# Scores of the cached K pages on TensorE from transposed pages, and the issue of K and V pages between the engines' steps

## The chip, the cores and the metric

One Trainium2 chip, one core. The metric is the device time of one execution of the program in microseconds. Three runs of the kernel before gave 4904.9 to 4907.69, median 4907.25.

## What is computed

One inference step of a two-layer trunk, for a prompt of 1024 tokens and for 8 samples of one new token each, with the same weights. Layer 0 has stick-breaking attention (part A) and an RWKV-7 mixing (part B) side by side. For each sample, part A reads a paged cache of 8192 earlier tokens: 64 pages of K and 64 of V, 128 tokens x 8 heads x 64 each, in float32 (256 KB a page), at places that a page table names.

```python
z = einsum('bthd,bshd->bhts', q, past_k) * DH ** -0.5 + bias      # scores, 8 heads, 8192 tokens
u = log_sigmoid(-z);  after = reversed cumsum of u, less u
w = exp(log_sigmoid(z) + after)
o = einsum('bhts,bshd->bthd', w, past_v)
```

Part B runs over the prompt in chunks of 64 tokens; each chunk has a small triangular system per head, and its state goes from chunk to chunk.

## The kernel before

All in float32 on tiles of 128 partitions. The program is a series of phases with a barrier after each: load, norm, Q and K, V, `pb_phase` (the 14 tiles of B's projection, each 72 matmuls of 344 columns in three groups), `attention_phase` (the prompt's attention), `rwkv_phase`, output projection, FFN, then layer 1. The cached pages of the 8 samples are worked on beside `pb_phase` (scores of sample 0) and `rwkv_phase`. The order on each engine is written out by hand; engines meet at semaphores alone.

K pages. SyncE issues one page after another into a ring of 8 buffers (`load_key_page`, L1021: wait until the buffer is free, load the page's number from the table, issue). The query of a sample is turned once on TensorE, stored to DRAM and loaded back as a row on all partitions (`start_sp`, `load_q`). VectorE forms the scores of two pages in a unit (`keys_dve`, L1110): a product of 128 x 1024 with the query (L1119), then a sum over 64 within each head (L1123). After 32 units `bias_dve` adds the bias for all pages of the sample.

V pages. ScalarE issues them one by one into a ring of 8 (`load_values`, L1076, called from `fetch`), between its own steps. TensorE adds each page with the weights of its 128 tokens (8 columns) to one of four column positions of bank 7 (`values_pe`, L1050, L1058), in any gap where `more(n)` stands. Scores become weights through `logs_act`, `softplus_dve`, `sums_pe`, `exponents_dve`, `weights_act`; the four positions are added up by `fold_act`, `select_pe`, `pick_act`.

`rwkv_phase` has 8 pairs of chunks. In pair i the V pages of sample i and the K pages of sample i + 1 are handled; the last pair has no K pages. A pair is: the preparation (`prep_act`, `prep_dve`, `prep_pe`; first exponential L1535, decays L1570), `prepped`, the transposes (L1692), the spread copies (L1801), the Gram products (L1700), the copies of the transposes (L1804 to 1808), five levels of the solve (`solve_levels_*`: a product, its copy y on ScalarE at L1415, one or two more products, an update on VectorE; VectorE has four units of K per level, TensorE four V pages in each of two gaps, ScalarE's queue eight page issues after each copy of y), two halves of the state's recurrence (L1729 to 1753), the copy of o (L1824), the fold (L1098) and the end of the pair with four V pages for the next one. The first seven pairs are a loop.

In `pb_phase` SyncE loads the weights of tile t + 2 when the row work of tile t is done (`mixed`; the same buffer holds mu), ScalarE rounds them (L248), VectorE forms the rest (L253) and, after two units of K pages, does the row work (L936 to 939).

## Time and profile before

| | us |
|---|---|
| median of 3 runs | 4907.25 (4904.9 to 4907.69) |
| profiled execution: device time | 4906.5 |
| profiled execution: span | 4904.6 |
| busy in the span: PE matmul | 3996.3 (81%) |
| DVE | 2586.6 (53%) |
| ACT | 1226.2 (25%) |
| POOL | 242.0 (5%) |
| page products L1119 and sums L1123 on DVE | 316.2 + 312.9 |
| V products L1058 on PE | 381.2 |
| `pb_phase` | about 236 to 457 |
| `rwkv_phase` | 723 to about 1925 |

PE is TensorE's matmuls, DVE VectorE, ACT ScalarE, SP SyncE; a q behind the name is the engine's queue of instructions, where DMAs are issued and registers computed. A row of a timeline is: start in us from the span's start, length, engine, line, operation, written tile <- read tiles, shape, count, and in brackets the idle time before it and what ended it. Neighbouring instructions of one kind are merged into one row, whose length goes from the first start to the last end. A float32 matmul shows as two records. PEclk is the granted clock of TensorE as a share of full speed, 2.4 GHz.

### The profile page before, as it was taken

To read this page: it belongs to the slowest core of one execution; us is meant where nothing else is said; L and a number is where in the kernel's file an instruction comes from. 1 tells how busy PE (TensorE), PEld (TensorE's weight loads), DVE (VectorE), ACT (ScalarE), POOL (GpSimd) and SP (SyncE) were. 2 spreads that over 40 slices of the span, in tenths; PEclk is the share of its full clock that TensorE was granted. 3 is DMA by queue.
4 is the path that set the end of the run, shared out by engine and by line. 5 is a ranking of instruction groups with operands and counts; after the bars stand their busy time and mean duration, and the time that the engine had idled before them with its cause. 6 is when DMAs were issued, how large, how long until landed. Compare 5 with 4: busy or idle time off the path is not lost. (4 is left out here: it accounts for less than half of the span.)

```text
span 4904.6 us, 82685 instructions
## 1 busy us (share of the span) xinstructions
PE 3996.3 (81%) x29517; PEld 3334.2 (68%) x29517; DVE 2586.6 (53%) x3393; ACT 1226.2 (25%) x1915; POOL 242.0 (5%) x302
## 2 busy tenths in 40 slices
PE   6786887666667774699998969995887876999998
PEld 6685323233333333699998959994777766999998
DVE  2156887777888744234334425554666423433443
ACT  3211551122111122222223322232222212222232
POOL 0000000000000000000000000001011000000000
PEclk8898998877789876899999989996877888999999
DMA  2253007766787751311114532322111132111254
GB/s 94 70 156 121 26 33 261 232 216 221 234 276 253 243 168 64 121 44 43 44 43 144 160 116 88 94 82 81 32 36 44 54 138 78 43 45 50 74 159 137
DMA packets 288462, 566.18 MB, mean 115 GB/s; under 512 B 41425, under 2 KB 107345, under 8 KB 281658
## 3 DMA queue, kind: packets, MB, share of 16 engines
q1 hardware_dynamic: 182186, 375.32, 24.0%
q10 hardware_dynamic: 90000, 141.65, 9.0%
q0 software_dynamic: 16032, 45.92, 2.4%
q8 instruction: 157, 2.57, 0.2%
q14 instruction: 87, 0.71, 0.0%
HBM read 504.38 MB, written 58.79 MB: 115 GB/s over the span
## 5 line engine op out<-in xcount | busy, mean ns | idle before, releaser
L261 PE MATMUL ps<-ffn_hh,up_wh 128*128 128x344 f32 x2112 | 677.9, 321 | 59.5 <-DVE up_wl L253 59.5
L263 PE MATMUL ps<-ffn_hl,up_wh 128*128 128x344 f32 x2112 | 676.3, 320 | 0.0
L262 PE MATMUL ps<-ffn_hh,up_wl 128*128 128x344 f32 x2112 | 675.5, 320 | 0.0
L1058 PE MATMUL ps<-pg_v,pg_w 128*8 128x512 f32 x1024 | 381.2, 714 | 156.7 <-DMA pg_v<-in_v_pages 106.6
L261 PEld LDWEIGHTS ps<-ffn_hh,up_wh 128*128 128x128 f32 x2112 | 398.2, 189 | 60.5 <-issue 60.5
L262 PEld LDWEIGHTS ps<-ffn_hh,up_wl 128*128 128x128 f32 x2112 | 398.2, 189 | 0.0
L263 PEld LDWEIGHTS ps<-ffn_hl,up_wh 128*128 128x128 f32 x2112 | 398.1, 188 | 0.0
L459 PE MATMUL ps<-down_ah,down_wh 128*128 128x344 f32 x1056 | 345.4, 327 | 48.1 <-DVE down_al L495 28.7
L1119 DVE TENSOR_TENSOR pg_prod<-pg_k,pg_q 128x1024 f32<-128x1024 f32 x256 | 316.2, 1235 | 47.7 <-DVE rw_mxt L1430 13.5
L461 PE MATMUL ps<-down_al,down_wh 128*128 128x344 f32 x1056 | 339.1, 321 | 0.0
L460 PE MATMUL ps<-down_ah,down_wl 128*128 128x344 f32 x1056 | 338.9, 321 | 0.0
L1123 DVE TENSOR_REDUCE pg_z<-pg_prod 128x16 f32<-128x1024 f32 (+1 forms) x256 | 312.9, 1222 | 11.4
L253 DVE TENSOR_TENSOR down_wl<-down_w,down_wh 128x1408 fp32r<-128x1408 f32 x96 | 155.9, 1624 | 308.4 <-ACT down_wh L248 308.4
L1058 PEld LDWEIGHTS ps<-pg_v,pg_w 128*8 128x8 f32 x1024 | 45.5, 102 | 391.2 <-DMA pg_v<-in_v_pages 310.9
L261 PE MATMUL ps<-hh,odd_wh 128*128 128x344 f32 x792 | 254.4, 321 | 31.7 <-DVE odd_wl L253 31.7
L262 PE MATMUL ps<-hh,odd_wl 128*128 128x344 f32 x792 | 253.8, 320 | 0.0
L263 PE MATMUL ps<-hl,odd_wh 128*128 128x344 f32 x792 | 253.8, 320 | 0.0
L459 PEld LDWEIGHTS ps<-down_ah,down_wh 128*128 128x128 f32 x1056 | 199.7, 189 | 62.2 <-issue 50.8
L248 ACT ACTIVATE down_wh<-down_w 128x1408 fp32r<-128x1408 f32 x96 | 132.4, 1379 | 379.5 <-PE ps L461 351.7
L460 PEld LDWEIGHTS ps<-down_ah,down_wl 128*128 128x128 f32 x1056 | 200.7, 190 | 0.0
L461 PEld LDWEIGHTS ps<-down_al,down_wh 128*128 128x128 f32 x1056 | 199.9, 189 | 0.0
L664 DVE TENSOR_TENSOR ffn_a<-up_cv,ps 128x344 f32 (+1 forms) x132 | 67.4, 511 | 246.7 <-PE ps L263 246.7
(430 smaller groups left out, 7463.8 us busy)
## 6 DMA issues: line engine op xcount, KB each, us to landing
pg_k<-in_k_pages SPq DMA_DIRECT2D x512, 256.0 KB, 4.5
pg_v<-in_v_pages ACTq DMA_DIRECT2D x512, 256.0 KB, 4.6
down_w<-in_w_down SPq DMA_DIRECT2D x96, 704.0 KB, 4.2
up_w<-in_w_ff SPq DMA_DIRECT2D x44, 1034.0 KB, 4.9
odd_w<-in_w_odd SPq DMA_DIRECT2D x33, 512.0 KB, 3.8
scratch_odd_rows<-odd_cv POOLq DMA_DIRECT2D x32, 516.0 KB, 2.9
dn_x<-scratch_odd_rows SPq DMA_DIRECT2D x8, 1536.0 KB, 7.7
scratch_x<-out_x POOLq DMA_DIRECT2D x16, 516.0 KB, 2.9
```

Source lines behind the costliest of these rows:

```text
L248: act.activation(hi, w, ACT.Copy).then_inc(rounded, 1)
L253: dve.tensor_tensor(lo, w, hi.bitcast(F32), ALU.subtract).then_inc(rest_ready, 1)
L261: pe.matmul(out, wh, xh, start=(k == 0), stop=False)
L262: pe.matmul(out, wl, xh, start=False, stop=False)
L263: mm = pe.matmul(out, wh, xl, start=False, stop=(k == n - 1))
L459: pe.matmul(ps[:, j, 0:GC], wh[:, v, wk], ah[:, kk, :], start=(kk == 0), stop=False)
L460: pe.matmul(ps[:, j, 0:GC], wl[:, v, wk], ah[:, kk, :], start=False, stop=False)
L461: mm = pe.matmul(ps[:, j, 0:GC], wh[:, v, wk], al[:, kk, :], start=False, stop=(kk == FT - 1))
L664: dve.tensor_tensor(a[:, bass.ds(2 * i + j, 1), col].rearrange("p a t -> p (a t)"), cv[:, j, col], ps[:, 3 + c, 0:GC], ALU.mult).then_inc( ...
L1058: pe.matmul(self.T.ps[c:c + H_A, 7, :], wts[:, :, g], self.vp[:, n, :], start=(g < 4), stop=(g >= NPG - 4), tile_position=(0, c), skip_gro ...
L1119: dve.tensor_tensor(self.prod[:, :, :], self.kp[:, n:n + 2, :], self.q[:, :].unsqueeze(1).to_broadcast([P, 2, D_A]), ALU.mult).then_inc(se ...
L1123: dve.tensor_reduce(z.rearrange("p h n -> p n h"), self.prod[:, :, :].rearrange("p n (h d) -> p n h d", h=H_A), AX.X, ALU.add).then_inc(se ...
```

## The change

K pages lie transposed in DRAM: for each page 128 channels of a head pair on the partitions, four such blocks, 128 tokens in a row (`k_pages` of `layouts`); the bytes of a page and its 2 KB per partition are the same. The query is kept as a block matrix of 32 columns per channel block (`qa`, `qb`). TensorE forms the scores of eight pages in a *round* (`keys_pe`): four channel blocks one after another, in each four matmuls with 256 moving columns in four column positions, into bank 6. ScalarE copies 128 x 256 (`scores_act`), TensorE transposes them back in two parts (`turn_pe`), VectorE adds the bias (`bias_dve`, eight short ones per sample).

SyncE issues K pages by rounds into a ring of 16, with one wait for eight pages. ScalarE issues V pages in *groups* of four with one wait for four, and TensorE waits for all four of a group. The places of groups, rounds and turns in each engine's order are new; the loops of `pb_phase` are unrolled. In `rwkv_phase` several tiles share memory (yw with rw, ya with ra, eN with L, eX with t1, o, oc and rs with L, nm and t2), and V's ring is allocated there. The core of the diff:

```diff
-            with sp.Fori(1, NB_T // 2) as i:
+            sp.wait_ge(pages.table_in, 16)
+            pages.load_keys(sp, 0, 0)
+            for i in range(1, NB_T // 2):
                 weights(i, 0)
-                keys(i)
+                pages.load_keys(sp, 0, i)
                 weights(i, 1)
-            keys(NB_T // 2)
+            pages.load_keys(sp, 0, NB_T // 2)
...
-            with pe.Fori(0, NB_T // 2) as i:
+            for i in range(NB_T // 2):
                 for j in range(2):
                     pe.wait_ge(w_split, 2 * i + j + 1)
                     for c in range(GRP):
                         pe.wait_ge(row_in, 6 * i + 3 * j + c + 1)
                         group_products(pe, T, 3 * j + c, wh[:, j, :], wl[:, j, :], c).then_inc(product, 1)
+                    if j == 0:
+                        pages.keys_pe(pe, 0, i)
+                    else:
+                        pages.turn_pe(pe, 0, i)
+            pages.keys_pe(pe, 0, NB_T // 2)
+            pages.turn_pe(pe, 0, NB_T // 2)
...
-            with act.Fori(0, LAST) as i:
+            pages.start_act(act)
+            for i in range(LAST + 1):
                 tile(i, 0)
-                tile(i, 1)
-            tile(LAST, 0)
-            tile(LAST, 1, True)
+                pages.scores_act(act, 0, i)
+                tile(i, 1, i == LAST)
+            pages.scores_act(act, 0, LAST + 1)
...
-
-                first, units = (RING // 2 * j, RING // 4) if i is not LAST else (0, RING // 2)
-                for n in range(units):
-                    pages.keys_dve(dve, 0, i if i is not LAST else LAST + j, first + 2 * n)
                 dve.wait_ge(row_in, 6 * i + 3 * j + 3 + 6)
...
+    def load_keys(self, sp, b, r):
+        at = NPG * b + self.ROUND * r
+        sp.wait_ge(self.k_used, at + self.ROUND)
+        for n in range(self.ROUND):
+            slot = self.ROUND * (r % 2) + n
+            sp.dma_start(self.kp[:, slot, :, :], self.T.io["k_pages"][self.page(sp, at + n), :, :, :]
+                         .rearrange("a p c t -> (a p) c t")).then_inc(self.k_in[r % 2], 16)
+
+    def load_values(self, sp, b, q):
+        at = NPG * b + self.GROUP * q
+        sp.wait_ge(self.v_used, at + self.GROUP)
+        for n in range(self.GROUP):
+            sp.dma_start(self.vp[:, self.GROUP * (q % 2) + n, :], self.T.io["v_pages"][self.page(sp, at + n), :, :]
+                         .rearrange("a p n -> (a p) n")).then_inc(self.v_in[q % 2], 16)
...
+    def keys_pe(self, pe, b, r):
+
+
+        if r == 0:
+            pe.wait_ge(self.q_ready, b + 1)
+            if not (isinstance(b, int) and b == 0):
+                pe.wait_ge(self.z_ready, b)
+        if not (isinstance(b, int) and b == 0 and r == 0):
+            pe.wait_ge(self.biased, 8 * b + r)
+        pe.wait_ge(self.k_in[r % 2], 512 * b + 128 * (r // 2) + 128)
+        alone(pe, self.passed)
+        first = self.ROUND * (r % 2)
+        for c in range(4):
+            for j in range(4):
+                mm = pe.matmul(self.T.ps[32 * j:32 * j + 32, 6, 0:2 * PAGE], self.qb[:, c, :],
+                               self.kp[:, first + j:first + self.ROUND:4, c, :], start=(c == 0), stop=(c == 3),
+                               tile_position=(0, 32 * j), skip_group_check=True)
+        mm.then_inc(self.k_used, self.ROUND)
+
+    def turn_pe(self, pe, b, r):
+
+        pe.wait_ge(self.z_copied, 8 * b + r + 1)
+        for n in range(2):
+            mm = pe.transpose(self.T.ps[:, 6, (2 + n) * P:(3 + n) * P], self.zt[:, n * P:(n + 1) * P], self.T.const("ident"))
+        mm.then_inc(self.z_turned, 1)
...
+        for q in groups:
+            if q == 0:
                 pe.wait_ge(self.w_ready, b + 1)
-            n, c = g % self.RING, 32 * (g % 4)
-            pe.wait_ge(self.v_in[n], 16 * self.loads * b + 16 * (g // self.RING) + 16)
-            pe.matmul(self.T.ps[c:c + H_A, 7, :], wts[:, :, g], self.vp[:, n, :], start=(g < 4), stop=(g >= NPG - 4),
-                      tile_position=(0, c), skip_group_check=True).then_inc(self.v_used, 1)
+            pe.wait_ge(self.v_in[q % 2], 512 * b + 64 * (q // 2) + 64)
+            alone(pe, self.passed)
+            for j in range(self.GROUP):
+                mm = pe.matmul(self.T.ps[32 * j:32 * j + H_A, 7, :], wts[:, :, self.GROUP * q + j],
+                               self.vp[:, self.GROUP * (q % 2) + j, :], start=(q == 0), stop=(q == NPG // self.GROUP - 1),
+                               tile_position=(0, 32 * j), skip_group_check=True)
+            mm.then_inc(self.v_used, self.GROUP)
...
+    def next_q_act(self, act, b):
+        act.wait_ge(self.k_used, self.RING + NPG * b)
+        act.activation(self.qb[:, :, :].rearrange("p c x -> p (c x)"),
+                       self.qa[:, bass.ds(b, 1), :, :].rearrange("p a c x -> p (a c x)"), ACT.Copy).then_inc(self.q_ready, 1)
+
+    def scores_act(self, act, b, r):
+        act.wait_ge(self.k_used, self.RING + NPG * b + self.ROUND * (r + 1))
+        act.activation(self.zt[:, :], self.T.ps[:, 6, 0:2 * P], ACT.Copy).then_inc(self.z_copied, 1)
 
     def logs_act(self, act, b):
...
             act.sem_inc(S["k_rn"], 1)
-            if sample is not None:
-                fetch(12)
             act.wait_ge(S["l_ready"], i + 1)
             act.activation(cut(t["eL"], n), cut(t["L"], n), ACT.Exp, scale=-DECAY)
             act.activation(cut(t["eN"], n), cut(t["L"], n), ACT.Exp, scale=DECAY)
...
             pe.matmul(ps[:, 3, 0:4 * n], halves, cut(t["t1"], n), start=True, stop=True).then_inc(S["k_sum"], 1)
-            more(8)
+            more(2)
             pe.wait_ge(S["rkk"], i + 1)
             pe.matmul(ps[:, 4, 0:4 * n], halves, cut(t["t2"], n), start=True, stop=True).then_inc(S["bonus"], 1)
-            more(4)
+            more(1)
...
@@ -1681,9 +1680,19 @@
         @block.tensor
         def _(pe):
             pe.wait_ge(S["lora_in"], 16)
-            def pair(i):
-                read = iter(range(NPG))
+            def pair(i, keys=True):
+                read = iter(range(NPG // Pages.GROUP))
                 more = lambda n: pages.values_pe(pe, i, [g for _, g in zip(range(n), read)])
+                score = lambda r: pages.keys_pe(pe, i + 1, r) if keys else None
+                turn = lambda r: pages.turn_pe(pe, i + 1, r) if keys else None
+
+                def between(n):
+                    more(1)
+                    if n % 2:
+                        score(n // 2 + 1)
+                    else:
+                        turn(n // 2)
+
                 prep_pe(pe, i, W, sample=i, more=more)
                 pe.wait_ge(S["prepped"], i + 1)
                 pe.wait_ge(S["gate_copied"], i + 1)
@@ -1709,8 +1718,10 @@
                 pe.wait_ge(S["spread"], 3 * i + 3)
                 gram(3, t["K"], Rx)
                 gram(4, t["B"], Rx)
-                more(4)
-                solve_levels_pe(pe, T, S, i, mtl, xm, xt, y, (5, 2, 1), S["pe_passed"], lambda: more(4))
+                more(1)
+                score(0)
+                slots = iter(range(10))
+                solve_levels_pe(pe, T, S, i, mtl, xm, xt, y, (5, 2, 1), S["pe_passed"], lambda: between(next(slots)))
...
                         mm = pe.matmul(ps[q(hd), 4, oc_(hd // 2)], u[r, hc(hd)], rb[r, hc(hd)], start=False, stop=True,
                                        skip_group_check=True)
                     mm.then_inc(S["mixed"], 1)
-                    more(4)
+                    turn(5 + p)
+                    more(1)
+                    score(6 + p)
                 finish_pe(pe, i, o[:, :, :], W)
+                turn(7)
                 pages.select_pe(pe, i)
...
         @block.scalar
         def _(act):
             act.preload_act_table_set(EXP_LN_SET)
+            pages.load_values(act, 0, 0)
+            pages.load_values(act, 0, 1)
             act.dma_start(X[:, :, :], xs[:, :, 0:W]).then_inc(S["xs_in"], 16)
             act.wait_ge(S["cleared"], 1)
...
                         last = act.activation(dst[r, :, e, :], src[r, :, :], ACT.Copy)
                     last.then_inc(S["spread"], 1)
+                pages.load_values(act, i, 2)
+                pages.load_values(act, i, 3)
                 act.wait_ge(S["turned"], i + 1)
                 act.activation(ktm[:, :], ps[:, 5, :], ACT.Copy)
...
-                fetch(20)
-                solve_levels_act(act, T, S, i, y, (5, 2, 1), lambda lv: fetch(20 + 8 * lv))
+                pages.load_values(act, i, 4)
+                scores(0)
+                pages.load_values(act, i, 5)
+
+                def between(lv):
+                    pages.load_values(act, i, 2 * lv + 4)
+                    scores(lv)
+                    if lv < 5:
+                        pages.load_values(act, i, 2 * lv + 5)
+
+                solve_levels_act(act, T, S, i, y, (5, 2, 1), between)
                 for p in range(2):
                     r = slice(64 * p, 64 * p + 64)
                     act.wait_ge(S["w_done"], 2 * i + p + 1)
                     act.activation(r0[r, :], ps[r, 0, :], ACT.Copy).then_inc(S["w_copied"], 1)
                     act.wait_ge(S["u_done"], 2 * i + p + 1)
                     act.activation(u[r, :], ps[r, 5, :], ACT.Copy).then_inc(S["u_copied"], 1)
-                    fetch(NPG)
+                    if p == 0:
+                        pages.load_values(act, i, 15)
+                        scores(6)
                 act.wait_ge(S["mixed"], 2 * i + 2)
                 act.activation(o[:, :, :], ps[:, 4, :].rearrange("p (k w) -> p k w", k=4), ACT.Copy)\
                    .then_inc(S["o_copied"], 1)
+                scores(7)
+                if more_samples:
+                    pages.load_values(act, i + 1, 0)
+                    pages.load_values(act, i + 1, 1)
...
                 dve.sem_inc(S["masked"], 1)
-                solve_levels_dve(dve, T, S, loop, i, xm, xt, (5, 2, 1), lambda lv: more(1 if lv == 1 else 4))
+                solve_levels_dve(dve, T, S, loop, i, xm, xt, (5, 2, 1), lambda lv: bias(lv - 1))
...
                     last.then_inc(S["h_ready"], 1)
+                    bias(5 + p)
                 assert loop.n == 20, loop.n
-                more(1)
-                finish_dve(dve, i, o[:, :, :], W, h[:, 4:8, bass.ds(i * W, W)], more)
-                more(NPG)
+                finish_dve(dve, i, o[:, :, :], W, h[:, 4:8, bass.ds(i * W, W)])
+                bias(7)
```

## Rows read from the trace of the kernel before

**Rows 1.** Stages: length; busy (count) of PE, PEld, DVE, ACT, POOL; PEclk, DMA share, GB/s.

```profile
236.00:457.00 221.00, 172.79 (x1012) 168.76 (x1012) 129.32 (x120) 30.88 (x57) 15.63 (x30) 0.90 0.48 145
876.00:1023.00 147.00, 100.99 (x936) 49.17 (x936) 115.38 (x123) 26.44 (x50) 8.05 (x5) 0.83 0.73 238
924.00:982.00 58.00, 49.60 (x540) 18.15 (x536) 49.26 (x45) 2.99 (x5) 0.00 (x0) 1.00 0.96 329
1755.00:1858.00 103.00, 83.97 (x924) 42.46 (x923) 30.62 (x47) 21.60 (x37) 7.09 (x5) 0.91 0.54 156
```

**Rows 2.** Part 5 of the page: the page operations on DVE.

```profile
L1119 DVE TENSOR_TENSOR pg_prod<-pg_k,pg_q 128x1024 f32<-128x1024 f32 x256 | 316.2, 1235 | 47.7 <-DVE rw_mxt L1430 13.5
...
L1123 DVE TENSOR_REDUCE pg_z<-pg_prod 128x16 f32<-128x1024 f32 (+1 forms) x256 | 312.9, 1222 | 11.4
```

**Rows 3.** Timeline of ACT, then of DVE, in the projection of B.

```profile
259.06 0.46 ACT L907 ACTIVATE pb_row<-ps 128x344 f32<-128x344 f32 x1 [3.33 <-PE ps L263]
266.59 1.06 ACT L248 ACTIVATE pb_wh<-pb_w 128x1024 fp32r<-128x1024 f32 x1 [7.07 <-DMA pb_w<-in_w_pb]
...
270.40 0.46 ACT L907 ACTIVATE pb_row<-ps 128x344 f32<-128x344 f32 x1 [2.05 <-PE ps L263]
...
260.89 1.29 DVE L939 SCALAR_TENSOR_TENSOR pb_xs<-pb_xs,pb_w,pb_row 128x1032 f32<-128x1032 f32 x1
267.69 1.23 DVE L253 TENSOR_TENSOR pb_wl<-pb_w,pb_wh 128x1024 fp32r<-128x1024 f32 x1 [5.50 <-ACT pb_wh L248]
...
450.39 1.29 DVE L939 SCALAR_TENSOR_TENSOR pb_xs<-pb_xs,pb_w,pb_row 128x1032 f32<-128x1032 f32 x1
```

**Rows 4.** Timeline of ACT in the second pair, then one row of DVE.

```profile
877.61 0.31 ACT L1535 ACTIVATE rw_th<-rw_xs 64x128 f32<-64x128 f32 x1 [8.23 <-issue]
...
881.25 3.92 ACTq L1080 DMA_DIRECT2D pg_v<-in_v_pages  x4
...
911.17 0.60 ACT L1804 ACTIVATE rw_mktm<-ps 128x512 f32<-128x512 f32 x1
...
924.38 0.60 ACT L1415 ACTIVATE rw_my<-ps 128x512 f32<-128x512 f32 x1 [11.14 <-PE ps L1390]
...
970.37 0.60 ACT L1415 ACTIVATE rw_my<-ps 128x512 f32<-128x512 f32 x1 [11.12 <-PE ps L1390]
...
1005.11 0.60 ACT L1824 ACTIVATE rw_o<-ps 128x512 f32<-128x512 f32 x1 [3.01 <-PE ps L1753]
1007.05 2.39 ACT L1098 ACTIVATE pg_fold<-ps 8x512 f32<-8x512 f32 x4 [1.34 <-PE ps L1058]
...
1016.37 4.24 ACTq L1080 DMA_DIRECT2D pg_v<-in_v_pages  x4
1024.08 0.31 ACT L1535 ACTIVATE rw_th<-rw_xs 64x128 f32<-64x128 f32 x1 [8.31 <-issue]
...
904.70 0.69 DVE L1583 TENSOR_TENSOR rw_A<-rw_kk,rw_eX 128x512 f32<-128x512 f32 x1 [2.74 <-ACTq L1574]
```

**Rows 5.** Timeline of PE in the same pair.

```profile
907.31 0.66 PE L1692 MATMUL ps<-consts,rw_K 128*128 128x128 f32 x4 [0.93 <-DVEq L1631]
...
987.62 1.07 PE L1058 MATMUL ps<-pg_v,pg_w 128*8 128x512 f32 x8
995.71 1.97 PE L1729 MATMUL ps<-rw_Hx,rw_A 128*64 128x128 f32 x8 [7.02 <-DVE rw_Hx L1889]
...
1005.00 1.91 PE L1058 MATMUL ps<-pg_v,pg_w 128*8 128x512 f32 x8
```

**Rows 6.** Timeline of ACT at the start of the RWKV stage.

```profile
723.13 0.45 ACTq L1783 DMA_DIRECT2D rw_xs<-scratch_xs_rows  x1
...
731.59 0.31 ACT L1535 ACTIVATE rw_th<-rw_xs 64x128 f32<-64x128 f32 x1 [7.19 <-DMA rw_xs<-scratch_xs_rows]
```

**Rows 7.** Instructions of one line of ACT's queue: duration ns min/median/max.

```profile
L1078 ACTq ALU_OP  x26: 35/35/35, 924.4 to 959.8; - x26
```

**Rows 8.** V pages, 924 to 982 us: from issue to landing.

```profile
DMA to landing us min/median/max: 3.1/4.9/6.2
```

189 lines of the change are left out of this document (65 added, 124 removed).

## The prediction

> **What bounds the kernel now.** I read the busy time and the clock by stage first [rows 1], then the costliest groups [rows 2], then the timelines of the two stages that the change touches: the projection of B (`pb_phase`, 236 to 457 us) and the eight pairs of chunks of `rwkv_phase` (from 723 us). Nothing outside them is edited, so I take the rest of the span as it is.
>
> In `pb_phase` the reader should see a chain, not a full engine: PE is busy for 173 of 221 us. DVE ends the row work of a tile at 260.89 + 1.29 = 262.2. Only then is its weight buffer free; the next weights are there for ACT at 266.59, their rest starts at 267.69 and ends at 268.9, and then come two page operations and two reductions (5.1, with gaps 5.3) before 2.65 us of row work [rows 3, 2]. That makes 4.4 + 2.3 + 5.3 + 2.65 = 14.65 us. The measured period is (450.39 - 260.89) / 13 = 14.58. PE itself needs 270.40 - 259.06 = 11.34 us for a tile. So 5.3 us of page work on DVE sits in the chain of every tile.
>
> In `rwkv_phase` a pair takes 1024.08 - 877.61 = 146.5 us, of which DVE is busy 115. Between the levels of the solve DVE handles four units of two pages, 4 x (1.24 + 1.22) = 9.8 us and gaps. But two other things are nearly as full there. The DMA engines are at 0.96 with 329 GB/s in 924 to 982 us [rows 1]; at 1.00 that is 343 GB/s, and 16 pages of 262,144 bytes (8 of K, 8 of V in each level) take 12.2 us at it. And ACT's queue issues four pages in 3.92 us, (3.92 - 0.35) / 3 = 1.19 a page, 9.5 us for the eight of a level [rows 4]. The levels run at (970.37 - 924.38) / 4 = 11.5 us. Taking DVE away therefore exposes DMA and ACT's queue at once.
>
> **The change, part by part.** All times are for the profiled execution, whose device time is 4906.5 us around a span of 4904.6; the median of the runs shown is 0.75 us above it.
>
> *Projection stage.* The 32 page units go from DVE to PE: eight rounds of scores and eight of turns. The price of a round: four pages of V abreast, 512 columns each, take 1.07 us at full clock (2.4 GHz) and 1.91 at half (1.2 GHz) [rows 5]. A round makes four steps, each four abreast with 256 columns, so 4 x 0.535 = 2.1 us (3.8 at half). Bounds: 1.7, if the start of the group is paid once, and 8.5, if the four don't run abreast; I take 2.1, since the row has the same tile positions. Two turns of 128 x 128: four take 0.66 us with their start [rows 5], so 0.4 for two. With page work gone the weight chain is 4.4 + 2.3 us, ready 6.7 us after a tile's row work, while PE reaches that tile 8.6 us after it (11.34 + 0.4 - 0.46 - 2.65). So PE is late next. Tile 0 ends as before at 259.06; then 13 x 11.34 + 7 x 2.1 + 6 x 0.4 = 164.5 gives 423.6, and 3.1 us of copy and row work 426.7, against 451.7 now [rows 3]. **-25.0 us** (-15 if the weights arrive 0.8 us a tile late, -28 with rounds of 1.7). The last round, copy, turn and bias (about 3.5 us) lie beside the store of the last tile. What SyncE issues before a tile's weights, eight pages in 9.3 us, is done before the 12.6 us of a tile are over. The extra copies for q (eight and one) come between ACT's first two roundings, some 3 us in a tile that has 11.
>
> *Start of the RWKV stage.* X was issued first, at 723.13, and the first exponential ran at 731.59 [rows 6]. Now eight V pages stand before it on ACT's queue: 8 x 1.1 = **+8.7 us**, once. Nothing else can run meanwhile.
>
> *A pair, from its first exponential to the first copy of y* (before: 924.38 - 877.61 = 46.8). The four pages issued ahead of the decays go; DVE idled 2.74 us for that [rows 4]: -2.7. But groups 2 and 3 are now issued between the spread copies and the copies of the transposes, while PE reads group 2 before it transposes. ACT's queue is free 0.7 us before the spreads end; the fourth page is issued 4.0 us later (0.66 to the first, then 3 x 1.11: a page costs 1.19 now and loses the register step for its wait, 0.035 and as much of a gap, [rows 4, 7]), lands 3.1 us later (the minimum, [rows 8]), the group takes 1.9 at half clock since PE has idled, the twelve transposes 1.6 at full and 2.4 at half. So the first copy, which followed the spreads directly at 911.17, comes 10.8 us later: +10.8 - 2.7 = +8.1. From there 2.4 us of copies, 0.6 for X, 4.5 for group 4, 2.2 for the first round of scores, 4.5 for group 5: 14.2 instead of 924.38 - 911.17 = 13.2. Sum **+9.1** (+6.5 at full clock, +11).
>
> *Four level steps* (46.0 before). The new loop goes through all engines: group of V issued on ACT's queue (4.0 to the fourth page), landing, V group on PE (1.1), scores (2.1), copy on ACT and the next issue (0.3): 7.5 + landing. The median landing of a V page in the levels is 4.9, the shortest 3.1 [rows 8]; with 4.7 the loop is 12.2 us, which is also what 16 pages need at 343 GB/s. Behind the scores' wait on ACT's queue stand the next group's issue and the copy of y, for which PE waits. 4 x 12.2 = 48.8: **+2.8** (-2.4 at a landing of 3.4, where PE's own 10.9 us bound; +8.8 at the maximum of 6.2).
>
> *From the last copy of y to the copy of o* (1005.11 - 970.37 = 34.7). PE waited 7.0 us for DVE's page units before the second half, and that half ran at half clock (9.3 us; by the ratio of 1.07 to 1.91 for its matmuls, about 6.0 at full) [rows 5, 4]: -10.3. About 3.4 us of waiting for single pages go and 2.5 for a round and turn come. **-11.2**. *From there to the next pair* (19.0): round 7 holds ACT 3.7 us, then eight page issues 8.9, fold 2.4, rstd, select and pick 2.3, the turn of the loop 1024.08 - 1020.61 = 3.5: 20.8, **+1.8**.
>
> A pair: 9.1 + 2.8 - 11.2 + 1.8 = +2.5 us, seven pairs **+17.5**. The eighth pair has no keys and its levels are ACT's queue alone, 8.7 us against some 10, but it pays the late transposes: **-3**.
>
> SyncE's K pages: a round of eight is asked for when the round two before it is used, and lands 14 us later, within two loops; hidden while the loop is over 8 us. The bias on DVE (eight short ones) and the copies on ACT lie beside PE's work.
>
> Sum: -25.0 + 8.7 + 17.5 - 3 = -1.8 us, 4904.7 in the profiled execution, 4905.5 as a median. I say **4905 us**.
>
> **A rule against the change.** In [rows 5] the V group of 987.62 starts without idle behind 64 x 64 products, so going from one tile shape to another costs nothing visible there; I put zero. The Trainium skill's page TensorEngine Tiling (Array Packing), Key Properties, says that changing the tiling mode drains TensorE. Each round of scores brings two such changes more. [...]
>
> **Rivals.**
> *A: the loop closes faster.* For it: V alone landed sooner than K and V together, and K's ring is now twice as deep. Against it: 16 pages per level stay 16. At the PE bound of 10.9 us with full clock in the first part, a pair is 5.2 + 2.6 better than my sum: -1.8 - 55 = 4851; halfway, which I find likelier, about 4878.
> *B (slower): landings grow because K and V now come in bursts that start at the same signal.* SyncE and ACT both start issuing when a round is used; each asks for about 230 GB/s, 460 together against 343. It decides from a mean landing above 5.1 us for a group's last page: every further microsecond costs 4 x 7 = 28 us. At 6.2 us: +42, 4947. PE at half clock inside the levels (it works about 8 of 12.2 us there, the granted clock was 1.00 before) would add 1.7 us a loop by the scores alone, +48.
> *C: the scores don't run four abreast*, so the change doesn't do what it says: 6.4 us more for each of 64 rounds, about +400.
>
> **How the numbers follow.** Forecast (within some 20 us of 4905): 0.45; this is spread evenly over its width, half of it within 0.2%, a quarter on each side. A: 0.28. B: 0.25. C: 0.02. About 0.2% (9.8 us) is what a measurement of this kernel can tell from no change. Faster 0.28 + 0.12 = 0.40; same 0.23; slower 0.25 + 0.10 + 0.02 = 0.37. The range goes from the better half of A, 4862, to B's 4950. The forecast's own range is 4885 to 4925.
>
> **What would show it.** Projection stage: tiles 11.4 and 13.4 us apart in turn, last row work near 427. First exponential of the RWKV stage near 716 (25 earlier, 9 later). PE waiting for the landing of group 2 before the transposes, 7 us or more, in every pair. Copies of y 12 us apart, ended by a PE that waited for V pages. Groups of scores 2.1 us. Pairs of 149 us with DVE busy under 45. I am wrong if the copies of y come 11 us apart (A), if landings pass 6 us (B), or if a round takes over 3 us at full clock (C).

## The result and the profile after

The changed kernel takes 4919.31 us (median of 12 runs, 4908.6 to 4932.08), the kernel before 4904.24 us beside it; the ratio is 1.0041 with a 95% interval of 1.0028 to 1.0055. So it is slower by 0.4%, where I had forecast no change at 4905 us. One of the twelve executions of the kernel before took 12192.57 us; the ratio is that of the means without it (4921.5 over 4901.1 us, 20 us apart), and the median of the other eleven is 4903.59. The time lies in my range (4862 to 4950), and on the side to which I gave 0.37.

The profiled execution of the changed kernel took 4908.6 us, the lowest of its twelve, around a span of 4906.6: only 2.0 us above that of before. That pair of profiles hides the loss. The lengths of the stages, from the first transfer of each in either trace:

| stage | before | after | |
|---|---|---|---|
| `pb_phase` | 221.3 | 193.7 | -27.6 |
| attention of the prompt (not edited) | 264.0 | 265.2 | +1.2 |
| `rwkv_phase` | 1203.2 | 1247.7 | +44.5 |
| DeltaNet stage (not edited) | 622.6 | 609.8 | -12.8 |
| all the rest (not edited) | 2593.5 | 2590.2 | -3.3 |

The 12.8 us of the DeltaNet stage are not the change's. In the fourteen profiles of this study, which all have that stage word for word, it is 609.6 to 609.8 us long in three and 618.5 to 622.6 in eleven, and the granted clock parts them: 0.79 to 0.80 in the three, 0.77 in the eleven. The stage before and after, columns as in [rows 1]:

```profile
3322.00:3944.60 622.60, 486.92 (x6157) 430.48 (x6157) 348.95 (x352) 154.68 (x177) 61.82 (x41) 0.77 0.18 50
...
3337.25:3947.00 609.75, 470.24 (x6157) 415.76 (x6157) 347.57 (x352) 154.63 (x177) 63.33 (x41) 0.80 0.18 51
```

Without it the edited stages say +17 to +18 us, the medians say +15 and the means +20.

The page of the changed kernel: the busy line (against DVE 2586.6 before), and the V products on PE, now waiting 217.5 us for V pages (106.6 in the same row of the page of before). The last row is the K pages' issue, its size, and the median from issue to landing.

```profile
PE 3915.1 (80%) x31689; PEld 3386.9 (69%) x31689; DVE 1973.3 (40%) x2937; ACT 1254.8 (26%) x1994; POOL 237.5 (5%) x303
...
L1062 PE MATMUL ps<-rw_vp,pg_w 128*8 128x512 f32 x1024 | 174.7, 766 | 267.4 <-DMA rw_vp<-in_v_pages 217.5
...
pg_k<-in_k_pages SPq DMA_DIRECT2D x512, 256.0 KB, 4.9
```

By stages, columns as in [rows 1]: the projection, the second pair, its level steps, the last pair.

```profile
238.00:432.00 194.00, 179.53 (x1280) 169.46 (x1280) 55.02 (x64) 37.62 (x74) 15.57 (x31) 0.96 0.52 164
867.00:1016.00 149.00, 91.19 (x1208) 59.10 (x1208) 38.69 (x66) 29.71 (x59) 7.13 (x5) 0.79 0.69 233
913.00:965.00 52.00, 35.98 (x605) 23.44 (x594) 7.82 (x15) 3.92 (x8) 2.66 (x3) 0.87 0.95 329
1763.00:1860.00 97.00, 55.38 (x696) 33.25 (x698) 31.32 (x48) 19.85 (x39) 7.09 (x5) 0.73 0.47 137
```

In a pair DVE falls from 115 to 39 us, as the change says, and the pair is longer: in the levels all engines now have idle time, while the transfer engines are where they were, 0.95 and 329 GB/s against 0.96 and 329 [rows 1].

The projection, which went well: the last row operation of tiles on DVE (against [rows 3]), and one round of scores and one turn on PE.

```profile
259.90 1.30 DVE L935 SCALAR_TENSOR_TENSOR pb_xs<-pb_xs,pb_w,pb_row 128x1032 f32<-128x1032 f32 x1
273.29 1.29 DVE L935 SCALAR_TENSOR_TENSOR pb_xs<-pb_xs,pb_w,pb_row 128x1032 f32<-128x1032 f32 x1
284.84 1.30 DVE L935 SCALAR_TENSOR_TENSOR pb_xs<-pb_xs,pb_w,pb_row 128x1032 f32<-128x1032 f32 x1
...
422.92 1.29 DVE L935 SCALAR_TENSOR_TENSOR pb_xs<-pb_xs,pb_w,pb_row 128x1032 f32<-128x1032 f32 x1
...
271.27 0.38 PE L1044 MATMUL ps<-consts,pg_zt 128*128 128x128 f32 x2
282.90 1.93 PE L1035 MATMUL ps<-pg_k,pg_qb 128*32 128x256 f32 x32
```

The start of the RWKV stage (against [rows 6]): ACT and its queue, then SP's queue. X is issued behind eight V pages and is there 13.6 us later, among the 16 K pages that SP issues from 698.29 on; the first exponential runs 22.4 us after the stage's start at 696.9 instead of 8.5.

```profile
697.85 7.83 ACTq L1013 DMA_DIRECT2D rw_vp<-in_v_pages  x8
705.71 0.46 ACTq L1799 DMA_DIRECT2D rw_xs<-scratch_xs_rows  x1
...
719.35 0.31 ACT L1542 ACTIVATE rw_th<-rw_xs 64x128 f32<-64x128 f32 x1 [12.58 <-DMA rw_xs<-scratch_xs_rows]
...
698.29 18.32 SPq L1006 DMA_DIRECT2D pg_k<-in_k_pages  x16
```

The level steps of the second pair: ACT and its queue, then PE, then the landings of V pages in 913 to 965 us.

```profile
913.95 0.38 ACT L1095 ACTIVATE pg_zt<-ps 128x256 f32<-128x256 f32 x1 [5.49 <-PE ps L1035]
914.76 3.84 ACTq L1013 DMA_DIRECT2D rw_vp<-in_v_pages  x4
918.64 0.60 ACT L1412 ACTIVATE rw_my<-ps 128x512 f32<-128x512 f32 x1 [4.32 <-issue]
919.95 4.02 ACTq L1013 DMA_DIRECT2D rw_vp<-in_v_pages  x4
926.58 0.38 ACT L1095 ACTIVATE pg_zt<-ps 128x256 f32<-128x256 f32 x1 [7.34 <-PE ps L1035]
...
923.74 1.06 PE L1062 MATMUL ps<-rw_vp,pg_w 128*8 128x512 f32 x8 [1.56 <-DMA rw_vp<-in_v_pages]
924.60 1.93 PE L1035 MATMUL ps<-pg_k,pg_qb 128*32 128x256 f32 x32
926.45 1.15 PE L1387 MATMUL ps<-rw_mxm,rw_mtl 64*64 64x64 f32 x32
...
DMA to landing us min/median/max: 3.7/5.3/6.5
```

Read them as one ring, a chain of waits that comes back to its own start. The copy of the scores at 913.95 lets ACT's queue go on; the odd V group is issued from 914.76, its fourth page at 918.21 (914.76 + 3.84 - 0.39); it has landed at 923.74, 5.5 us later; PE reads it, forms the next round of scores from 924.60, and the copy at 926.58 closes the ring: 0.81 + 3.45 + 5.53 + 0.86 + 1.98 = 12.63 us. The same terms taken over all 28 level steps of the seven pairs have the means 0.81 + 3.51 + 5.71 + 0.98 + 2.09 = 13.10 us (5.57 of the third is the landing itself), which is the mean step of 13.1. No engine is full in it. The copy of y at 918.64 stands behind the issue (4.32 us idle, ended by "issue"), so the solve moves at the ring's pace.

Between the pieces of a pair (first exponential, first copy of a transpose, first and fifth copy of y, copy of o, next exponential) the traces give, as means over the seven pairs with keys, with the last pair and the median of the runs beside them; the second pair of the kernel before, on which my sum rested, has 33.6, 13.2, 46.0, 34.7 and 19.0. Runs e1 to e12 are told below; e9 is an edit of the kernel before. They were taken at three times, e1 to e4, e5 to e8 and e9 to e12, and the kernel before ran beside them at medians of 4900.3, 4901.8 and 4895.9 us, against 4904.2 beside the changed kernel, which ran at none of the three. So a difference in us between rows of different groups holds some 3 to 8 us that are no edit's; where that matters the ratios to the kernel before are given too (1.0041 for the changed kernel).

| kernel | exp to transpose | to y1 | four levels | to o | to next exp | pair | last pair | median |
|---|---|---|---|---|---|---|---|---|
| before | 32.8 | 13.6 | 47.0 | 33.6 | 18.3 | 145.3 | 111.4 | 4904.2 |
| after | 38.7 | 12.2 | 52.5 | 24.7 | 21.1 | 149.1 | 115.8 | 4919.3 |
| e1 small K transfers | 39.0 | 12.2 | 47.3 | 23.0 | 19.8 | 141.4 | 114.9 | 4848.7 |
| e2 quarter of the scores | 39.0 | 11.5 | 47.6 | 22.3 | 20.3 | 140.8 | 113.0 | 4849.1 |
| e3 V on GpSimd | 35.5 | 8.6 | 55.8 | 26.4 | 8.8 | 135.1 | 123.4 | 4810.6 |
| e4 X first | 38.9 | 12.4 | 53.2 | 24.6 | 21.2 | 150.1 | 114.7 | 4910.4 |
| e5 groups 2, 3 early | 35.4 | 12.4 | 53.1 | 25.2 | 21.0 | 147.1 | 110.7 | 4895.6 |
| e6 scores' copy last | 39.2 | 12.3 | 45.7 | 25.0 | 20.8 | 142.9 | 114.2 | 4875.7 |
| e7 V singly | 37.2 | 12.4 | 51.1 | 23.4 | 22.5 | 146.6 | 107.3 | 4891.4 |
| e8 GpSimd, spread | 36.3 | 8.8 | 42.4 | 30.7 | 10.2 | 128.4 | 112.0 | 4754.6 |
| e9 before, GpSimd, spread | 35.9 | 8.1 | 47.2 | 38.2 | 9.6 | 139.0 | 104.2 | 4850.0 |
| e10 ScalarE, all | 35.0 | 13.0 | 41.8 | 25.1 | 22.7 | 137.7 | 101.4 | 4814.6 |
| e11 next groups late | 38.6 | 12.4 | 51.9 | 24.6 | 22.2 | 149.7 | 110.2 | 4918.0 |
| e12 e8, scores earlier | 36.7 | 8.5 | 41.5 | 29.1 | 11.4 | 127.1 | 109.9 | 4745.8 |

### The profile page after: what moved, and what is told of

The parts are those of the page before. It is cut to its first block and busy times, and to the rows that moved or that the text cites. A ratio compares the mean times of both kernels' runs of the same rounds, so it can differ in the third digit from the quotient of the medians.

```text
span 4906.6 us, 84794 instructions
## 1 busy us (share of the span) xinstructions
PE 3915.1 (80%) x31689; PEld 3386.9 (69%) x31689; DVE 1973.3 (40%) x2937; ACT 1254.8 (26%) x1994; POOL 237.5 (5%) x303
## 5 line engine op out<-in xcount | busy, mean ns | idle before, releaser
L1062 PE MATMUL ps<-rw_vp,pg_w 128*8 128x512 f32 x1024 | 174.7, 766 | 267.4 <-DMA rw_vp<-in_v_pages 217.5
L1062 PEld LDWEIGHTS ps<-rw_vp,pg_w 128*8 128x8 f32 x1024 | 22.9, 109 | 309.0 <-issue 308.3
L261 PEld LDWEIGHTS ps<-hh,odd_wh 128*128 128x128 f32 x792 | 149.3, 189 | 32.4 <-issue 32.4
L253 DVE TENSOR_TENSOR up_wl<-up_w,up_wh 128x1024 fp32r<-128x1024 f32 x88 | 107.6, 1225 | 158.2 <-ACT up_wh L248 158.2
L601 ACT ACTIVATE up_row<-ps 128x344 f32<-128x344 f32 x132 | 60.5, 458 | 423.0 <-PE ps L263 423.0
```

Of the source, the lines that this page charges most:

```text
L253: dve.tensor_tensor(lo, w, hi.bitcast(F32), ALU.subtract).then_inc(rest_ready, 1)
L261: pe.matmul(out, wh, xh, start=(k == 0), stop=False)
L601: act.activation(row[:, j, 2 + c * GC:2 + (c + 1) * GC], ps[:, c, 0:GC], ACT.Copy)\
L1062: mm = pe.matmul(self.T.ps[32 * j:32 * j + H_A, 7, :], wts[:, :, self.GROUP * q + j], self.vp[:, self.GROUP * (q % 2) + j, :], start=(q == ...
```

## The experiments

The theory after the result: the work taken off DVE was not missed, but the level steps now run at a ring through ACT's queue, the landing of a V group, PE's read and scores, and the copy on ACT; and at four more places (X, group 2, the fold, the odd group) something waits behind V issues on ACT's queue. Rivals: total transfers set the steps; PE's clock sets them.

### e1: K transfers of an eighth

```diff
-            sp.dma_start(self.kp[:, slot, :, :], self.T.io["k_pages"][self.page(sp, at + n), :, :, :]
+            sp.dma_start(self.kp[0:rows, slot, :, :], self.T.io["k_pages"][self.page(sp, at + n), 0:rows, :, :]
...
-                        pages.load_keys(sp, i + 1, r)
+                        pages.load_keys(sp, i + 1, r, 16)
```

> In the RWKV stage each K page's transfer brings 16 of its 128 partitions only (an eighth of the bytes), so the scores formed there are not those of the reference; issues, waits, products and copies all stay. Theory (the level steps turn on a loop: V group issued on ScalarE's queue, landed, read on TensorE, scores behind it, copy on ScalarE, next group): the V landing of 5.4 us and group 2's wait of 10.26 us shrink with the traffic, a level step falls from 12.8 us toward the 10.0 us of the last pair, where ScalarE's eight issues and one copy fill it, the first X lands in about 8.4 us instead of 13.6 us; together 45 to 75 us off the changed kernel's time (about 4855). Rival 'the clock': the same step lengths, TensorE waits for nothing and works at half clock, under 10 us off. Rival 'the issues themselves': the time stays within 10 us too, since every issue is still there, but the landings fall to about 3 us; the clock alone doesn't tell these two apart, the waits do.

Measured: 4848.7 us, 70.6 below the changed kernel. The waits of PE in the second pair (total, times, longest), first of the changed kernel, then of e1; then e1's landings in the levels.

```profile
PE ps L1062 <- DMA rw_vp<-in_v_pages: 28.4, 11, 10.3
```

```profile
PE ps L1062 <- DMA rw_vp<-in_v_pages: 14.9, 6, 9.9
...
DMA to landing us min/median/max: 2.8/3.3/4.0
```

A landing falls by 2.0 us (5.3 to 3.3) and a level step by 1.3 (13.1 to 11.8), so the landing lies in the ring. The steps did not come to 10.0: in these two rows of ACT a ring takes 10.66 us, in others 11.9, where PE waits for a copy of y behind an issue. Over the 28 steps the last page of the odd group lands 3.34 us after its issue instead of 5.57, but PE now starts on it 1.01 us after the landing instead of 0.14: the way over the copy of y has become the later one.

```profile
913.62 0.38 ACT L1095 ACTIVATE pg_zt<-ps 128x256 f32<-128x256 f32 x1 [6.55 <-PE ps L1035]
...
924.28 0.38 ACT L1095 ACTIVATE pg_zt<-ps 128x256 f32<-128x256 f32 x1 [5.31 <-PE ps L1035]
```

And the longest wait, that for group 2 ahead of the transposes, stays at 9.9 us with small transfers: it is a wait for the issue.

### e2: a quarter of the scores' products

```diff
-        for c in range(4):
+        for c in range(4) if isinstance(b, int) and b == 0 else (0,):
```

> In the RWKV stage a round of scores is 4 products instead of 16 (one of four blocks of the head dimension; its scores are partial): TensorE's round falls from 1.93 us to about 0.5 us, K traffic and all waits stay. Theory (the copy of the scores stands in ScalarE's order ahead of the odd V group's issue, so the round lies in the loop): about 1 us off each of the four level steps and of the tail, 25 to 45 us in all. Rival 'transfers set the steps': the landing is late by as much, under 8 us off. Rival 'the clock': with less work the clock falls further and the time does not fall, or rises.

Measured: 4849.1 us, 70.2 below, more than expected (25 to 45). The steps fall by 1.2 us, near the 1.4 us that a round lost, with all transfers in place: scores lie in the same ring. The tail and the way to the next pair shorten by another 2.4 and 0.8 us, which I had left out. As K's bytes and PE's scores each give the same, neither is the bound by itself.

### e3: V pages issued by GpSimd

```diff
-                    pages.load_values(act, i, 2 * lv + 4)
...
+                for q in range(2, 4):
+                    pages.load_values(pool, i, q)
                 pool.wait_ge(S["blocks_copied"], i + 1)
                 for lv in range(1, 6):
                     pool.tensor_tensor(h8(mtl[:, lv - 1, :]), h8(mt[:, :]), m8(f"lev{lv}T"), ALU.mult)\
                         .then_inc(S["blocks_ready"], 1)
+                for q in range(4, 16):
+                    pages.load_values(pool, i, q)
+                if more_samples:
+                    pages.load_values(pool, i + 1, 0)
+                    pages.load_values(pool, i + 1, 1)
```

All other issues of V on ScalarE are taken out too, and GpSimd issues groups 0 and 1 of the first sample ahead of its loop.

> Only the place of the V issues changes: GpSimd's queue issues all V groups in the same order, with the same waits, ScalarE none; output unchanged. Theory (ScalarE's queue is in the loop, 8 issues of 1.15 us in every level step, 8.7 us ahead of the transposes' copies, 8.5 us ahead of the fold, and ahead of the first X): level steps to 9 to 11.5 us (what stays is issue, landing 5.4 us and product of a group, two groups in flight), th to ktm 38.7 to about 32, o to the next th 21.6 to about 15, start 22.5 to about 10: 80 to 140 us off, about 4810. Rival 'transfers set the steps': steps stay at 12.5 us, the start and the two other places still give 30 to 60 us. Rival 'GpSimd issues slower than ScalarE' (over 1.6 us a page, 64 pages in 149 us of which five block products take part): slower than the changed kernel by 50 us or more.

Measured: 4810.6 us, 108.7 below the changed kernel and 1.7% below the kernel before (0.9828, 0.9802 to 0.9853). The places where ScalarE's issues had stood shortened: exponential to transposes 35.5 (about 32 expected), to y1 8.6, o to the next exponential 8.8 instead of 21.1 (about 15 expected). The levels did not, with 14.0 us a step where 9 to 11.5 were expected; the tail (last copy of y to o) is 1.7 us longer, and the last pair 7.6 us. PE in the first two steps of the second pair:

```profile
877.96 1.15 PE L1387 MATMUL ps<-rw_mxm,rw_mtl 64*64 64x64 f32 x32
887.56 1.90 PE L1062 MATMUL ps<-rw_vp,pg_w 128*8 128x512 f32 x8 [8.46 <-DMA rw_vp<-in_v_pages]
889.40 0.69 PE L1044 MATMUL ps<-consts,pg_zt 128*128 128x128 f32 x2
890.02 1.97 PE L1398 MATMUL ps<-rw_my,rw_mxt 64*64 64x64 f32 x32
...
897.96 1.06 PE L1062 MATMUL ps<-rw_vp,pg_w 128*8 128x512 f32 x8 [0.46 <-DMA rw_vp<-in_v_pages]
```

Group 4 was issued behind GpSimd's five block products (7.15 us), so the first step waits 8.46 us for it; without that, the eight groups between the first and the fifth copy of y come (55.8 - 8.5) / 8 = 5.9 us apart, near half the round trip of a ring of two groups (issue 4.9, landing 5, read 1: 5.5). The 8.5 is from one pair and the 55.8 a mean, so this is an estimate.

### e4: X ahead of the V pages

```diff
-            pages.load_values(act, 0, 0)
-            pages.load_values(act, 0, 1)
             act.dma_start(X[:, :, :], xs[:, :, 0:W]).then_inc(S["xs_in"], 16)
+            pages.load_values(act, 0, 0)
+            pages.load_values(act, 0, 1)
```

> Only the first X transfer of the RWKV stage moves ahead of the eight V pages of the first two groups in ScalarE's queue; output unchanged. Theory: X is issued about 8 us earlier and lands with the first K pages only; the first exp starts 8 to 14 us earlier (22.5 us after the stage's start now, 8.5 us before the change), and as groups 0 and 1 are not needed until the weights are ready, all of it stays: 8 to 14 us off the changed kernel. Rival 'the 16 K pages of SyncE alone delay it': X still takes 13 us to land and only the 8 us of issue come off, or groups 0 and 1 land late and give it back: under 5 us.

Measured: 4910.4 us, 8.9 below (against before 1.0016, 1.0004 to 1.0028, so 12 us by the ratios). The first exponential runs 10.5 us after the stage's start instead of 22.4, 11.9 us of gain; a pair is 1.0 us longer in this trace, which I can't tell from the scatter of single pairs (148.3 to 152.8 in the first six of the changed kernel).

### e5: groups 2 and 3 issued in the preparation

```diff
             act.sem_inc(S["k_rn"], 1)
+            pages.load_values(act, sample, 2)
...
             act.sem_inc(S["decays"], 1)
+            pages.load_values(act, sample, 3)
...
-                pages.load_values(act, i, 2)
-                pages.load_values(act, i, 3)
```

> Only the place of V groups 2 and 3 in ScalarE's order changes: group 2 is issued in the preparation after the exponential of the key norms, group 3 after the three decays, instead of both behind the six spread copies; output unchanged. Theory (TensorE's 10.3 us wait for group 2 ahead of the transposes is a wait for its issue, since it was 9.9 us in the run with small K transfers too, where a V landing took 3.3 us): that wait goes, the issue of 4.4 us delays the decays by at most 2 us, group 3's issue lies beside VectorE's four products; th to ktm falls from 38.7 to about 32 to 35, 25 to 45 us off over eight pairs. Rival 'the level steps take it back' (group 4 is no earlier, since group 3 is read after the Gram products): under 10 us off. Rival 'ScalarE's queue is in the preparation's chain of exponentials': no gain or slower by up to 20 us.

Measured: 4895.6 us, 23.7 below, just short of the 25 to 45 expected (0.9982, 0.9967 to 0.9997: 29 us by the ratios). Exponential to transposes falls by 3.3 us a pair, as expected; the levels take back 0.6; the last pair gives 5.1.

### e6: the odd group's issue ahead of the scores' copy

```diff
-                    scores(lv)
                     if lv < 5:
                         pages.load_values(act, i, 2 * lv + 5)
+                    scores(lv)
```

> Only one order on ScalarE changes: in each level step the odd V group is issued ahead of the copy of the scores instead of behind it, so that this issue doesn't wait for TensorE's round of scores; output unchanged. Theory (the round of scores lies in the loop through ScalarE's order, as the run with a quarter of the scores showed, which lost more than the 1.4 us a round in each pair): level steps 12.8 to 11 to 12 us, 20 to 45 us off the changed kernel. Rival 'the odd group's issue waits for the read of the group before it anyway, and that stands only one slot ahead of the scores': under 8 us off, and the turn waits for the later copy instead.

Measured: 4875.7 us, 43.6 below the changed kernel and faster than the kernel before (0.9941, 0.9924 to 0.9958), from one line moved. All of it is in the levels: 11.4 us a step instead of 13.1. ACT's queue now issues eight pages in one go, then the copies; the level window of this run:

```profile
912.34 9.85 ACTq L1013 DMA_DIRECT2D rw_vp<-in_v_pages  x8
922.30 0.39 ACT L1095 ACTIVATE pg_zt<-ps 128x256 f32<-128x256 f32 x1 [10.19 <-issue]
922.58 0.60 ACT L1412 ACTIVATE rw_my<-ps 128x512 f32<-128x512 f32 x1
924.76 8.64 ACTq L1013 DMA_DIRECT2D rw_vp<-in_v_pages  x8
...
905.00:950.00 45.00, 32.84 (x538) 20.39 (x528) 7.08 (x13) 3.61 (x8) 3.40 (x3) 0.82 1.00 356
```

This parts the rivals. The bytes of a step are what they were, the clock is lower (0.82 against 0.87), and the steps are shorter; so neither the transfer engines' rate nor the clock was the bound of the changed kernel's steps. (The clock still lengthens single steps, as told further below.) Only now is the transfer side full: 1.00 and 356 GB/s, 16 pages in 11.8 us.

### e7: V pages singly again

```diff
-        sp.wait_ge(self.v_used, at + self.GROUP)
         for n in range(self.GROUP):
+            sp.wait_ge(self.v_used, at + n + 1)
...
-            pe.wait_ge(self.v_in[q % 2], 512 * b + 64 * (q // 2) + 64)
-            alone(pe, self.passed)
             for j in range(self.GROUP):
+                pe.wait_ge(self.v_in[self.GROUP * (q % 2) + j], 128 * b + 16 * (q // 2) + 16)
...
-            mm.then_inc(self.v_used, self.GROUP)
+                mm.then_inc(self.v_used, 1)
```

The increment of a semaphore ahead of a group (`alone`) goes too.

> The V pages keep their places and their ring of eight, but have a semaphore and a wait each again: TensorE reads a page as soon as it lands, ScalarE issues a page as soon as its slot is read, instead of four by four; output unchanged. Theory (two groups in flight, a slot idle from its landing to the landing of the group's last page, 3.4 us): the round trip shortens by up to 3 us, level steps fall by 0.5 to 2 us, 15 to 50 us off. Rival 'ScalarE's queue issues in order at 1.1 us a page and the last page of a group lands when it did': within 8 us. The other side: 16 more waits in a pair and the switch of TensorE between tile sizes at more places give 10 us more.

Measured: 4891.4 us, 27.9 below (0.9986, 0.9967 to 1.0005). The steps give 0.35 us each, less than expected; group 2's wait gives 1.5 us a pair and the tail 1.3, the way to the next pair takes 1.4 back, and the last pair gives 8.5 us, once. Taking four pages under one wait was itself a loss of about 0.6%.

### e8: GpSimd's issues earlier, V groups spread

The lines on GpSimd (`pages.load_values(pool`) are shown against e3, whose edits are all in place.

```diff
                 def between(n):
-                    more(1)
+                    if n not in (3, 7):
+                        more(1)
...
+                    more(1)
                     pe.wait_ge(S["w_copied"], 2 * i + p + 1)
...
-                for q in range(2, 4):
+                for q in range(2, 5):
                     pages.load_values(pool, i, q)
...
                         .then_inc(S["blocks_ready"], 1)
+                    pages.load_values(pool, i, lv + 4)
```

> V issues on GpSimd's queue as in the run before (4810.6 us), with two more edits: group 4 and its followers are issued ahead of and between the five block products, and TensorE reads two of the ten groups of the level steps in the tail instead (slots 3 and 7 left out, one more group beside each copy of w); output unchanged. Theory (with ScalarE free the level steps are a row of V groups, each half a round trip of issue 4.9 us, landing 5 us and reading 1 us, 55 us for ten of them): levels about 44 us instead of 55 us, tail (y5 to o) up by at most 3 us: about 8 us a pair and 50 to 80 us off 4810.6, about 4750. Rival 'total transfers' (the K pages and V pages of a pair, 33.5 MB, at the 327 GB/s of the level steps would need 102 us of 135 us): the steps shorten but the landings grow, 15 to 30 us off. Rival 'the clock': TensorE below full speed in the levels fills the steps, under 15 us off.

Measured: 4754.6 us against "about 4750": 3.1% below the kernel before (0.9693, 0.9677 to 0.9709). Levels 42.4 us (44 expected, though by a count of ten groups for eight where the four copies of y enclose eight and now six), tail +4.3 (at most 3 expected). The first step's wait for group 4 has gone, and in the levels the transfers are at 0.95 again, as the rows below show. The clock is not excluded as a limit of these shorter steps: 13 of the 28 rounds of scores in the levels take 2.6 to 3.7 us instead of 1.93, at a granted clock of 0.50 to 0.72, against three in the changed kernel.

```profile
867.44 1.06 PE L1062 MATMUL ps<-rw_vp,pg_w 128*8 128x512 f32 x8 [0.79 <-DMA rw_vp<-in_v_pages]
...
866.00:913.00 47.00, 33.90 (x596) 20.83 (x594) 6.95 (x13) 3.96 (x10) 19.73 (x31) 0.86 0.95 336
```

### e9: the same two edits on the kernel before

```diff
-                solve_levels_pe(pe, T, S, i, mtl, xm, xt, y, (5, 2, 1), S["pe_passed"], lambda: more(4))
+                slots = iter(range(10))
+                solve_levels_pe(pe, T, S, i, mtl, xm, xt, y, (5, 2, 1), S["pe_passed"],
+                                lambda: more(0 if next(slots) in (3, 7) else 4))
...
+                    more(4)
                     pe.wait_ge(S["w_copied"], 2 * i + p + 1)
...
+                for g in range(8, 20):
+                    pages.load_values(pool, i, g)
                 pool.wait_ge(S["blocks_copied"], i + 1)
...
+                    for g in range(4 * lv + 16, 4 * lv + 20):
+                        pages.load_values(pool, i, g)
...
-                fetch(20)
```

Every other issue of V on ScalarE is taken out as well.

> The kernel before, with its scores still on VectorE, and the two edits of the fastest run so far (V issues on GpSimd's queue ahead of and between the block products, slots 3 and 7 of the levels left out and one read more beside each copy of w); V pages singly, output unchanged. It asks whether the change itself is worth anything once ScalarE's queue is free. Theory: VectorE's page units (four of about 2.3 us in a level step, with its own two or three operations) keep the steps at 11 to 11.5 us and the pb stage at 221 us; only the places where ScalarE's issues stood (ahead of the fold and behind the pick, in the preparation) shorten, by 4 to 9 us a pair: 4830 to 4870, which is 75 to 115 us above 4754.6 of the same edits on the changed kernel. Rival 'the V route is everything, the scores' engine nothing but the pb stage': 4754.6 + 27.6 = about 4782.

Measured: 4850.0 us, in the middle of what the theory gave; 95.4 us above e8 (0.9912 against 0.9693: 107 us by the ratios). The steps stay at 11.8 us and the projection stage at 219.6. DVE is busy for 42.9 of 47.1 us in the levels of the second pair, which fits its page units as the bound; no run took them out of e9. So the change as a whole (scores on PE, rounds, groups) is worth 95 to 107 us (2.0 to 2.2%) once V's issue has left ACT's queue, and cost 15 us with the issues on that queue in the order of the change; another order on the same queue turns that into a gain (e6, e10).

### e10: all of it with ScalarE's issues

The edits of e4 to e7, and

```diff
+                pages.fold_act(act, i)
+                finish_act(act, i, W)
                 if more_samples:
                     pages.load_values(act, i + 1, 0)
+                pages.pick_act(act, i)
+                if more_samples:
                     pages.load_values(act, i + 1, 1)
-                pages.fold_act(act, i)
-                finish_act(act, i, W)
-                pages.pick_act(act, i)
```

> The changed kernel with V issues still on ScalarE and all edits of that kind together: X first, groups 2 and 3 in the preparation, the odd group's issue ahead of the scores' copy, a wait for each page, and of the next sample's two groups one behind the exponential of the variance and one behind the pick; output unchanged. Each of the first four alone gave 9, 24, 44 and 28 us against 4919.3 us, 105 us if they added up. Theory: the last three shorten one loop and ScalarE's eight issues of 1.1 us and one copy fill 10 us of a level step as in the last pair, so they add up to less: levels 10 to 11 us a step, th to ktm 35 us, o to the next th about 17 us, 75 to 115 us off, 4805 to 4845, and well above the GpSimd version. Rival 'ScalarE's queue was no bound, only the order in it': 105 us off or more, at 4800 or below.

Measured: 4814.6 us (0.9832, 0.9816 to 0.9849), 104.7 below the changed kernel. It lies in the theory's range. Whether the parts add up can't be said: with e11's 1.3 they are 105.4 by the medians, but 114 against 102 by the ratios, and five single gains and losses, each known to some 6 to 9 us, are in that sum. The steps are 10.45 us, near what eight issues and the copies fill.

### e11: the next sample's groups behind the fold

The edit is the diff shown for e10, alone.

> Only the next sample's two V groups move in ScalarE's order: from ahead of the fold to behind the exponential of the variance and behind the pick; output unchanged. Theory (8.5 us of issue stand ahead of the fold and of the variance's logarithm, and o to the next th fell from 21.6 to 8.8 us when GpSimd issued them): group 0 now lies beside VectorE's five products, group 1 is still ahead of the next pair's first exponential, so about 4 us of the 12.8 us go in each of seven pairs: 20 to 35 us off 4919.3. Rival 'the issue lies on the path wherever it stands': under 8 us off.

Measured: 4918.0 us, 1.3 below (1.0047, 1.0029 to 1.0066, against 1.0041): no gain that can be told from none, the rival's case. The fold comes earlier, but the issues then stand ahead of the next pair's first exponential (o to the next exponential 22.2 against 21.1). Only another engine took them off the path (8.8 in e3).

### e12: e8 with the rounds of scores one place earlier

```diff
             pe.matmul(ps[:, 3, 0:4 * n], halves, cut(t["t1"], n), start=True, stop=True).then_inc(S["k_sum"], 1)
+            first[0]()
             more(2)
...
             more(1)
+            first[1]()
...
-                        score(n // 2 + 1)
+                        score(n // 2 + 2)
```

The two calls are score(0) and turn(0); copy, bias and the later turns move up with them.

> The fastest run (4754.6 us) with the rounds of scores one place earlier: the next sample's first round is formed in the preparation, while TensorE waits 6.2 us for the weights, its copy, turn and bias follow there, and each later round moves up one slot, so that the tail holds one round less; output unchanged. Theory (the levels run at 336 GB/s and 0.95 of the transfer engines' time, the preparation at 143 GB/s): eight K pages move from the levels' and the tail's traffic into the preparation, the K wait of 3.5 us in the fourth level goes, VectorE's last bias no longer holds up the next pair's logarithms (3.2 us): 3 to 7 us a pair, 20 to 50 us off 4754.6. Rival 'the V round trip alone sets the levels': only the 3.2 us at the pair's start, 10 to 20 us off. Other side: ScalarE's copy in the preparation lengthens th to ktm, by 0.7 us a pair.

Measured: 4745.8 us (0.969, 0.9674 to 0.9707), 8.8 below e8, but the kernel before was 6.0 us lower beside it too: by the ratios (0.9690 and 0.9693) 1.5 us, so the times don't show that e12 is the faster of the two. In any case it is less than the 20 to 50 expected, and than the rival's 10 to 20. In one profile of each the levels give 0.9 us and the tail 1.6, the way to the next pair takes 1.2 back, where I had expected to win 3.2. Why it does was not followed up.

## Why the prediction was wrong, point by point

**What bounds the kernel now** held: DVE could be taken away, and what then set the time was ACT's queue and the transfers together. The ring that joins them was in the sum, and it was mis-sized. Three terms of the sum failed: the landing in the level steps, the level steps of the last pair, where the wait for four pages was put at nothing, and the landing of the first X.

**Projection stage**: -25.0 forecast, -27.6 measured, last row work at 424.2 instead of 426.7. Tiles are 13.39 and 11.55 us apart in turn, as forecast; a round takes 1.93 us (2.1 said), a turn 0.38 (0.4).

**Start**: +8.7 forecast, +14.0 measured. X is issued 8.8 us after the stage's start, as I said (7.8 of it are the eight issues); the step that failed is that X was taken to land as before: from its issue to the first exponential it took 13.6 us instead of 8.4, among 16 K pages and 8 V pages. e4 takes 11.9 us of it back.

**First exponential to first copy of y**: +9.1 forecast for the second pair. There it went from 46.8 to 50.9, +4.1. The wait for group 2 came as described:

```profile
901.69 1.91 PE L1062 MATMUL ps<-rw_vp,pg_w 128*8 128x512 f32 x8 [10.26 <-DMA rw_vp<-in_v_pages]
...
906.39 0.60 ACT L1816 ACTIVATE rw_mktm<-ps 128x512 f32<-128x512 f32 x1 [9.29 <-PE ps L1701]
```

The copy comes 9.3 us behind the spreads (10.8 said), the preparation ahead of it is 4.1 us shorter (2.7 said), and the way to y1 12.3 us instead of 14.2.

**Level steps**: the step that decided. Forecast 12.2 us a step, 48.8 in all, +2.8. Measured 13.1 on the average (52.5), 51.1 in the second pair, +5.1 there and +5.5 on the average. The ring was the right one and over the 28 steps its terms are 3.51 us to the fourth page (4.0 said), 0.98 for the group (1.1), 2.09 for the scores (2.1), 0.81 from their copy to the next issue (0.3), and 5.71 from the issue of the group's last page to PE's start on it. This landing was taken as 4.7, below the median of [rows 8], with no row that asked for it. The two small misses of 0.5 cancel, by luck, and the landing's 1.0, less 0.1 on the group, is the step's 0.9. Rival B named this mechanism and its threshold, 5.1 us for a group's last page. 0.9 us a step in 28 steps are 25 us; as a difference it is 19, since the steps of before were 47.0 on the average and not the 46.0 of the second pair. e1, e2 and e6 show ring and landing each by its own edit. B's other half, PE below full speed in the levels, is there too, in a small part. Three of the 28 steps take 14.5 to 15.3 us, and in just these a round of scores takes 2.7 to 3.0 us at a granted clock of 0.64 to 0.72; one of them:

```profile
802.37 3.01 PE L1035 MATMUL ps<-pg_k,pg_qb 128*32 128x256 f32 x32
```

The other 25 have a mean of 12.9 us, so these three cost 0.2 us a step, some 6 us in all, by this trace. It isn't what bounds the steps: e6 has shorter ones at 0.82.

**Last copy of y to o**: -11.2 forecast, -9.5 in the second pair, -8.9 on the average. **To the next pair**: +1.8 forecast, +2.6 and +2.8. The eight issues ahead of the fold are the row to see:

```profile
999.05 8.53 ACTq L1013 DMA_DIRECT2D rw_vp<-in_v_pages  x8
1007.69 2.38 ACT L1112 ACTIVATE pg_fold<-ps 8x512 f32<-8x512 f32 x4 [9.07 <-issue]
```

**A pair**: +2.5 forecast, +3.8 measured (145.3 to 149.1), 26.7 us over seven against 17.5. The half-right terms cancel in part: transposes too dear by 4.6, levels too cheap by 2.7, tail by 2.3, the way on by 1.0.

**Last pair**: -3 forecast, +4.4 measured. The levels there are 40.1 us and not 35: ten us a step, as before. I had set 8.7 from the spacing of issues alone and left out the wait for four pages under one. After a copy of y ACT's queue waits until a whole group is read (from 1816.02 to 1818.21 in the rows below, then of e7, where the issue follows at once). With singly waited pages (e7) the levels are 35.1, although the same copies stand between the issues. So the levels are about 5 of the 7.4 us that this term misses.

```profile
1815.42 0.60 ACT L1412 ACTIVATE rw_my<-ps 128x512 f32<-128x512 f32 x1 [8.15 <-issue]
1818.21 8.00 ACTq L1013 DMA_DIRECT2D rw_vp<-in_v_pages  x8
...
1799.44 0.60 ACT L1411 ACTIVATE rw_my<-ps 128x512 f32<-128x512 f32 x1 [7.90 <-PE ps L1061]
1800.14 8.52 ACTq L1013 DMA_DIRECT2D rw_vp<-in_v_pages  x8
```

**Sum**: -1.8 forecast; the terms measured give -27.6 + 14.0 + 26.7 + 4.4 = +17.5, and the medians +15.1. The profile's own +2.0 would have looked like a hit, by the luck of a higher clock in the DeltaNet stage. The misses are 5.3 (start), 9.2 (pairs), 7.4 (last pair), less 2.6 (projection).

**The rule against the change** did not show. In the rows above a round of scores (tile 128 x 32) starts 0.86 us after a V group (128 x 8) whose own length is 1.06, and 64 x 64 products start 1.85 us after a round of 1.93: no gap on either side (the ends of matmuls are modelled in these profiles, so starts are compared). The Trainium skill's page TensorEngine Tiling (Array Packing), Key Properties, states that a change of tiling mode drains TensorE; this trace shows no time for it. V groups and scores stand at the same four column positions (`tile_position=(0, 32 * j)`), so only a change to another shape, such as the one from scores to 64 x 64, can have tested the rule; I had counted two changes a round. **Rival C** fell (1.93 us a round). **Rival A**, the loop that closes faster, is not what the change did; e6 and e10 reach such steps (11.4 and 10.45 us) by another order on ACT.

## What to carry to other kernels

When an engine is relieved, draw the ring that remains, through queue, landing, product and copy, with one measured row for each term, and take for a landing its value under the traffic that the ring itself makes, not one below the median. In a queue that runs in order, ask of every issue what it waits behind and what waits behind it: one copy moved behind four issues was worth 0.9%, and the whole change was worth 2.0% with the other transfers issued by GpSimd, and cost 0.4% with ScalarE's issues in its first order. Run the reference beside every group of runs: here it moved by up to 8 us between groups, as much as some of the edits seemed to give. And compare stage by stage: here an unedited stage hid most of the loss in the pair of profiles.

## What was unexpected of the hardware

- The transfer engines moved 356 GB/s at a share of 1.00 in e6's levels; from 329 at 0.96 I had worked out 343.
- GpSimd's queue issues a V page every 1.23 us, ScalarE's every (3.84 - 0.39) / 3 = 1.15 us in the rows above: hardly dearer, and the engine had little else to do. Behind its five block products GpSimd issued eight pages 0.53 us apart (880.00 to 883.74), and the last of them landed 8.0 us after its issue. Two rows of e3:

```profile
861.24 0.54 POOL L1013 DMA_DIRECT2D rw_vp<-in_v_pages  x1 [0.71 <-issue]
862.47 0.54 POOL L1013 DMA_DIRECT2D rw_vp<-in_v_pages  x1 [0.69 <-issue]
```

- The unedited DeltaNet stage has lengths near 610, 619 and 622 us from one execution to another, 13 us apart at most, nearly as much as this whole change moves the time. The short ones have a granted clock of 0.79 to 0.80 and PE busy for 470 to 472 us, the others 0.77 and 483 to 487. Why the clock differs from one execution to another is open.
